# The scaling of the attention probabilities moves from VectorE to GpSimd in a two-model kernel of one core

## What is computed

```python
# first block, 8 heads, 528 tokens (16 of them meta tokens)
s = jnp.einsum('bhqd,bhkd->bhqk', qb, kh).astype(jnp.float32) + (cb[..., :, None] - c[..., None, :])
s = jnp.where(kpos[None, :] <= qpos[:, None], s, -jnp.inf)
p = jax.nn.softmax(s, axis=-1)
return jnp.einsum('bhqk,bhkd->bhqd', p.astype(vh.dtype), vh)
...
# second block, windowed attention; the neighbourhood attention has a bias table and no sink
p = jax.nn.softmax(jnp.concatenate([s_win, s_ctx, s_sink], axis=-1), axis=-1).astype(q.dtype)
return (jnp.einsum('bhgqk,bkhd->bqhgd', p[..., :span], vb)
        + jnp.einsum('bhgqk,bkhd->bqhgd', p[..., span:span + kc.shape[1]], vc))
```

## Time and profile before

| | us |
|---|---|
| median of 3 runs | 3799.26 (3793.26 to 3802.93) |
| the profiled execution, device time | 3804.83 |
| its span in the trace | 3803.1 |
| attention of the first block | 648.4 to 706.0 |
| attention of layer 0, second block | 1520.5 to 1705.4 |
| attention of layer 1, second block | 2904.1 to 3036.0 |

### The profile page before, as it was taken

How to read it: one execution, slowest core, us unless ns; L and a number is a source line. 1 busy time by engine, 2 the same in 40 slices (tenths; PEclk the granted TensorE clock), 3 DMA queues, 4 the chain that set the end, 5 groups by cost and what they waited for, 6 DMA issues and landing times. The chain is left out here.

```text
span 3803.1 us, 40896 instructions
## 1 busy us (share of the span) xinstructions
PE 3129.0 (82%) x16584; PEld 1828.1 (48%) x16584; DVE 1295.1 (34%) x2679; ACT 542.4 (14%) x1050; POOL 16.3 (0%) x16
## 2 busy tenths in 40 slices
PE   6477688969999698988599999999398787888785
PEld 5345475558874365654433333333276543333332
DVE  1645314333320202895511111111705943111114
ACT  1100003321110200541100000000202520000000
POOL 0000000000000000000000000000000000000000
PEclk9677598989999899979699999999699988999998
DMA  3030130112222121430167777775320014999994
GB/s 122 8 144 12 67 144 34 51 45 78 78 83 73 57 70 45 156 111 11 45 234 269 263 264 264 263 264 209 117 66 34 1 56 177 340 350 350 335 350 161
DMA packets 239855, 551.63 MB, mean 145 GB/s; under 512 B 24273, under 2 KB 24785, under 8 KB 223857
## 3 DMA queue, kind: packets, MB, share of 16 engines
q1 hardware_dynamic: 239728, 549.89, 40.3%
HBM read 547.76 MB, written 2.10 MB: 145 GB/s over the span
## 5 line engine op out<-in xcount | busy, mean ns | idle before, releaser
L2337 PE MATMUL ps<-ring,xsL 128*64 128x512 f32 x2048 | 481.2, 625 | 93.2 <-DMA ring<-in_w_gate 78.9
L2337 PEld LDWEIGHTS ps<-ring,xsL 128*64 128x64 f32 x2048 | 148.0, 143 | 422.6 <-issue 306.5
L1589 PE MATMUL ps<-hT,ring 128*128 128x264 f32 x1408 | 313.5, 386 | 2.5 <-PEq L272 2.5
L1589 PEld LDWEIGHTS ps<-hT,ring 128*128 128x128 f32 x1408 | 267.4, 190 | 48.4 <-issue 2.7
L2337 PE MATMUL ps<-ring,htL 128*64 128x512 f32 x1024 | 225.0, 594 | 18.9 <-ACT htC L2509 9.5
L2467 DVE TENSOR_TENSOR tokens_a<-tokens_a,ps 128x512 f32<-128x512 f32 x108 | 74.2, 687 | 404.3 <-PE ps L2361 404.3
L286 PE MATMUL ps<-hT,ring 128*128 128x264 f32 x640 | 147.4, 394 | 23.8 <-DMA ring<-in_w 19.9
L1554 PE MATMUL ps<-ring,actT 128*128 128x512 f32 x352 | 154.2, 601 | 7.0 <-PEq L1577 7.0
L2467 DVE TENSOR_TENSOR tokens_b<-tokens_b,ps 128x512 f32<-128x512 f32 x72 | 49.5, 687 | 322.2 <-PE ps L2361 322.2
L2337 PEld LDWEIGHTS ps<-ring,htL 128*64 128x64 f32 x1024 | 73.3, 137 | 160.2 <-issue 160.2
L286 PEld LDWEIGHTS ps<-hT,ring 128*128 128x128 f32 x640 | 124.3, 195 | 47.1 <-DMA ring<-in_w 20.7
(11 more groups left out here) (481 smaller groups left out, 4017.0 us busy)
## 6 DMA issues: line engine op xcount, KB each, us to landing
ring<-in_w_gate SPq DMA_DIRECT2D x128, 1024.0 KB, 9.3
ring<-in_w_up SPq DMA_DIRECT2D x128, 1024.0 KB, 9.4
ring<-in_w_down SPq DMA_DIRECT2D x128, 1024.0 KB, 9.5
ring<-in_w SPq DMA_DIRECT2D x73, 1024.0 KB, 4.9
ring<-in_w_mod SPq DMA_DIRECT2D x48, 1024.0 KB, 5.0
h<-in_x SPq DMA_DIRECT2D x2, 2048.0 KB, 8.2
gb<-in_rows SPq DMA_DIRECT2D x8, 512.0 KB, 4.4
out_dram<-h SPq DMA_DIRECT2D x4, 512.0 KB, 2.6
```

The lines of the kernel that those rows point to most:

```text
L1589: mm = pe.matmul(k.ps[:, 4 * (j % 2) + 2 * gv + h, 0:HALF1], w(c_), hT[:, c_, h * HALF1:(h + 1) * HALF1], start=c_ == 0, stop=c_ == KD - 1 ...
L2337: mm = pe.matmul(k.ps[HD * par:HD * par + HD, bank + half, :], lhsL(4 * kh + kk, par), w[half][par][:, kk, :], start=kh + kk == 0, stop=kh ...
```

## The change

`normalise` on DVE keeps the reciprocal alone and raises a new signal, `inverse`. A program for GpSimd is added to the block of every attention stage: for each pair it waits for `inverse` and does the two multiplications, in the same buffers, of the same size, and each raises `probs` as before. DVE waits for `probs` of pair i-4 ahead of the reciprocal of pair i, since `rinv` has four places.

```diff
@@ -554,10 +555,9 @@
                     dve.wait_ge(exped.sem, exped.of(2 * i + 2))
-                    steps(dve.reciprocal(rinv[0:n, i % 4, :], rsum[0:n, i % 4, :]))
-                    for h in range(2):
-                        pr = prob[i % NB][0:n, h, 0:u["width"]]
-                        dve.tensor_scalar(pr, pr, rinv[0:n, i % 4, h:h + 1], None, ALU.mult).then_inc(probs.sem, 1)
+                    if i >= 4:
+                        dve.wait_ge(probs.sem, probs.of(2 * i - 6))
+                    dve.reciprocal(rinv[0:n, i % 4, :], rsum[0:n, i % 4, :]).then_inc(inverse.sem, 1)
@@ -583,6 +583,16 @@
+            @block.gpsimd
+            def _(pool):
+                for i in range(N):
+                    u = pairs[i]
+                    n = u["n"]
+                    pool.wait_ge(inverse.sem, inverse.of(i + 1))
+                    for h in range(2):
+                        pr = prob[i % NB][0:n, h, 0:u["width"]]
+                        pool.tensor_scalar(pr, pr, rinv[0:n, i % 4, h:h + 1], None, ALU.mult).then_inc(probs.sem, 1)
```

More of the change, by code:

```diff
@@ L448, in attention @@
     turned, pt_ready, out_ready, out_taken = sg["turned"], sg["pt"], sg["out"], sg["out_taken"]
+    inverse = sg["inverse"]
     N = len(pairs)
@@ L618, in attention @@
         s.close(2 * N)
-    for s in (scores, turned, pt_ready, out_ready, out_taken):
+    for s in (scores, inverse, turned, pt_ready, out_ready, out_taken):
         s.close(N)
@@ L2619 @@
            "multiplied", "used", "choice", "gath", "xs", "gatd", "gtr", "gts", "silu", "hid", "htr", "hts", "yes", "scat",
-           "added", "inner_v", "inner_s"]
+           "added", "inner_v", "inner_s", "inverse"]
 def program(nc, dram, out):
```

## The result

The changed kernel takes **3860.0 us** (median of 4 runs, 3857.7 to 3864.3), the kernel before it 3801.1 us beside it (4 runs): a ratio of 1.016, with a 95% interval from 1.014 to 1.018. It is slower by some 60 us, where 18 were forecast; the direction was right and the size was not.

A forecast was written before the change was run, and what follows sets the result against it. DVE was taken to bound both layers, with PE close behind in layer 0 and bounding the first block. Layer 0 +12, layer 1 +4 and first block +1.5 made about +18 on 3799.3: 3817 us, range 3772 to 3860.

The forecast's parts named there:

- What bounds the kernel: Attention stages: DVE fullest in both layers (167.3 of 184.9 us, 119.5 of 131.9); PE bounds the first block.
- What leaves DVE: Second block: the multiplications, 31.75 us in layer 0 and 24.4 us in layer 1; the reciprocal stays.
- The price p: One multiplication on GpSimd: 0.95 us for 640 elements, 1.10 for 768, 0.46 for 256, between memset-based bounds.
- Rival 3: GpSimd and convolution collide, multiplication at the upper price or above: +53 us, 3852 us, chance 0.20.
- if the multiplications are 1.3 us and more, the price is: Sign in GpSimd's multiplication times: at 1.3 us and more, the assumed price of 0.95 us for 640 is wrong.
- The new path, 0.97 + 2p: Layer 0, reciprocal to next `row_min` through two GpSimd multiplications and the transposes: 2.87 us for 640 keys.
- the prediction's own list of pairs: Layer 0: 16 narrower pairs, 5 with one convolution operation and 11 with two; 8 of 768 keys, 2 and 6.
- The collision: GpSimd's multiplication and the convolution's line 2115 take turns by whole instructions, 3 in 4; layer 0 +12 us.
- Rival 1: GpSimd and line 2115 run side by side without colliding: together -36 us, 3763 us, chance 0.19.
- Layer 1: Three buffers, so the path ends a pair's period before needed; collision +16 or -8 us, middle taken +4 us.
- The first block: PE hides the later second head, there after 1.82 us and needed at 2.22; masks cost +1.5 us.

The follow-up runs named there:

- price: The changed kernel with each GpSimd multiplication taking only the first 40% of the columns, the rest left unscaled: 3784.1 us.
- moved_two: The changed kernel with two probability buffers in layer 1 in place of three: layer 1 went from 145.5 to 174.3 us.
- late_take: The changed kernel with the convolution's operations ahead of `take` of the pair before on DVE, nothing left out: 3860.5 us.
- split_late: The kernel where DVE multiplies head 0 and GpSimd head 1, with the convolution's operations moved ahead of `take`: 3809.2 us.
- split: The changed kernel, but DVE multiplies head 0 and GpSimd head 1, each with its own signal to PE: 3791.4 us.
- split_tt: DVE multiplies head 0 and GpSimd head 1, GpSimd's multiplication written as a product of two tensors: 3830 us.

## Why the prediction was right or wrong

**What bounds the kernel** was read rightly: DVE in both layers, PE close behind in layer 0 and bounding the first block. **What leaves DVE** too: 144 and 104 us are within 9 us of what is left when the earlier trace rows are taken from the earlier trace rows (the convolution's operations, at 1091 and 873 ns on the mean, gave back 3.4 and 7.3).

**The price p is the step that failed.** Its upper bound, "the same twice, reading and writing one after the other", took the memset's 0.84 ns an element of the earlier trace rows for a pass of any kind, and two passes for the whole. The multiplication takes 2.5 ns, and p is 1.94 us where the bound had 1.26 and the middle 0.95. An operation that only writes gives no upper bound for one that computes on GpSimd, and DVE's 1.035 us of the earlier trace rows, the reason for the middle, is another engine's. Rival 3 had "the upper end or above", and its 3852 is the nearest number, but by luck: it was priced at 1.26 us and a collision of whole instructions, the one too low and the other too high. The sign for this step was rightly named, "if the multiplications are 1.3 us and more, the price is".

**The new path, 0.97 + 2p, held**, and its sum comes out in part by luck. With the measured p it gives 4.85 us for 640 keys in layer 0, against 5.06 in the timeline above and 2.98 and 3.98 in the earlier trace rows. Put through the prediction's own list of pairs it gives +9 for five narrow pairs with one operation, +10 for eleven with two, and for the eight of 768 keys (0.22 + 4.72 + 0.88 = 5.82 against 3.11 and 4.11) +16, so +35 us. The reciprocal of the 24th pair starts 169.1 us after the stage does, where it was 132.3: +36.8.

But the list takes all sixteen narrow pairs at 640 keys, and eight of them have 512; and the measured means hold what GpSimd lost to DVE. With each pair's own width, and the 1.57, 1.89 and 2.21 us that 512, 640 and 768 elements take undisturbed, the path alone gives an estimate of +24. GpSimd's multiplications lose 5 us to DVE's operations up to there. The 7 or so that are left were not separated; the work ahead of `turn` in PE's queue and PE's lower clock, told at the end, are candidates. The rest of layer 0's 42.8 us lies in the context pairs and behind them, where p for 256 elements is 1.1 us, not 0.46.

**The collision** was given 3 chances in 4, priced in whole instructions. At the forecast's p it would have made layer 0 longer by 12; price shows 1.6 less. It is there, but the step was mis-sized: the forecast had DVE wait for the end of a multiplication, and DVE waits for the end of its first third at most, which the convolution mostly misses. In the changed kernel it costs the convolution 0.06 us an operation in layer 0 and 0.12 in layer 1 on the mean, and GpSimd 9.1 and 3.8 us in all.

**The gain without a collision** was overrated as well. Rival 1 had -15 for layer 0 and -20 for layer 1; price gives -1.6 and -15.7. The window over layer 0's latent pairs in price, which answers to the fourth of the earlier trace rows:

```profile
1518.00:1664.00 146.00, 133.95 (x1468) 98.79 (x1468) 108.90 (x303) 75.77 (x136) 51.45 (x52) 0.95 0.51 172
```

PE is busy for 133.95 of 146 us, so it still has the 12 us of idle time that it had before, and it is not PE's work that took the gain. What ends its waits has changed: over the stage PE waits 9.1 us for `row_min` where it waited 17.1, and 10.1 at `turn` for GpSimd, which had no part in the stage. DVE in turn waits 13.9 us for `mix`, which stands behind `turn`, and 19.2 for the transposes. So at the forecast's p the new path and PE's queue already take back what DVE saves; rival 1 counted DVE's own way and PE's work, and not this.

**Layer 1** was thought safe: "with three buffers, this path ends a pair's period before it is needed". True of `row_min` (moved_two shows what it is worth, 28.8 us), but not of `take`. The prediction named `mix` as standing behind the waiting `turn` on PE, and added nothing for it in layer 0; it didn't follow it on to DVE, where `take` waits for it with the convolution queued behind. Taking the convolution from behind it gave 12.4 us back in late_take, against the 12.1 lost.

**The first block** was to cost 1.5 us, since PE would hide it. With 1.6 us for 528 elements the second head comes 3.4 us after the reciprocal, where the prediction had 1.82 and needed 2.22. PE waits (4.0 us for GpSimd in all), and the stage is 6.1 us longer.

## What to carry to other kernels

Before work goes from a full engine to an idle one, look for a row of that very form of instruction on the idle engine. Where there is none, an operation that only writes is no upper bound for one that computes, and the price should be let go to several times that of the engine it leaves. Then ask whose queue stands behind the new wait, and follow it for two steps and two turns of the loop: here the buffer was free in time, and the result behind it in PE's queue was not. Where two equal pieces of work must both be done before the next stage, giving the idle engine one of them puts its price on the path once and not twice; that alone turned a loss of 1.6% into a gain of 0.2%. And where two engines hold one another up, ask at which point of the one's instruction the other's begins: the same two kinds of operation cost each other little in the changed kernel and much in late_take and split_late, by their order alone.

## What the runs showed of the hardware

- GpSimd's multiplication by a scalar takes 0.29 us and 2.5 ns an element (0.93, 1.89 and 2.21 us for 256, 640 and 768), 3.4 times DVE's time for 640. A constant in place of the pointer saves 0.08 us. The same product with two tensor inputs takes 1.04 us for 512 and 1.47 for 768: the form with more inputs is faster by a third.
- GpSimd and an operation of DVE that reads two tensors of SBUF exclude one another, for the whole of DVE's operation but only for the first part of GpSimd's: 0.05 us and 0.84 ns an element of the scalar form (a third of it), 1.05 of 1.25 us of the two-tensor form at 640 elements. So the multiplication of 640 goes from 1.89 to 2.18 us in late_take, and the convolution's 1035 ns to 1149 there, 1270 in split_late and 1340 with the two-tensor form. DVE's multiplication of one tensor by a scalar is a party to it as well: it holds GpSimd's scalar form up (1.89 to 2.24 in split) and is held by the two-tensor form (0.55 to 1.65 in split_tt). What GpSimd does in the rest of its instruction no run tells.
- DVE's copy of two elements at the head of `row_min` takes 0.16 or 0.17 us in the kernel before, all 40 times. In the changed kernel four of them have a record of 0.43 to 0.65 us, but the operation behind starts 0.07 us later as always, so DVE lost nothing. In late_take it starts later in four places, 0.44 us behind a copy of 0.52. What sets these apart stays open.
- The granted clock of layer 0's stage fell from 0.86 to 0.80, and PE's busy time rose from 166.6 to 188.7 us for the same instructions, while PE waited 34.0 us at `turn` for GpSimd in 37 places. Up to the 24th reciprocal the clock is 0.86 where it was 0.94, and PE busy for 137.3 us where it was 121.5. How much of the 42.8 us this adds was not separated.
